# Low parts of two neighbouring ring slots in one VectorE operation, in the ten wide groups of a transformer layer pair

## What is computed

```python
h = sqrelu_mlp(rmsnorm(x, g), w1, w2)   # (256 x 8192) @ (8192 x 2048) is the second product
proj = h @ w_in                          # q, k, v: (256 x 2048) @ (2048 x 1024) each
```

## Time and profile before

| | |
|---|---|
| median of 3 runs | 1775.42 us |
| lowest, highest | 1775.01, 1775.8 us |
| span of the profiled execution | 1773.5 us |
| TensorE matmul busy | 1766.1 us |
| VectorE busy | 1277.0 us |
| ScalarE busy | 895.7 us |
| mean granted TensorE clock | 1.000 |

### The profile page before, as it was taken

One profiled execution on the slowest core, in us unless ns is written; L12 is line 12 of the kernel. 1 busy time (PEld: TensorE's weight loads), 2 busy tenths in 40 slices (PEclk: granted clock), 3 DMA queues, 4 the chain that ended last, 5 costly groups with the idle time before them and its releaser, 6 DMA issues.

```text
span 1773.5 us, 26289 instructions
## 1 busy us (share of the span) xinstructions
PE 1766.1 (100%) x8791; PEld 1497.5 (84%) x8791; DVE 1277.0 (72%) x1689; ACT 895.7 (51%) x1248; POOL 139.2 (8%) x190
## 2 busy tenths in 40 slices
PE   9999999999999999999999999999999999999999
PEld 7888888888888888888888887878888888888887
DVE  6567777556788788878887877898888655555654
ACT  7434444446556445545554455767644445553442
POOL 1012122000001000100000000020013011100000
PEclk9999999999999999999999999999999999999999
DMA  9564444555467656855775576565655554555554
GB/s 329 200 223 162 163 163 166 187 177 188 169 215 230 197 191 209 228 201 191 214 236 190 196 229 217 178 209 198 198 186 175 196 178 178 177 177 189 179 190 154
DMA packets 99116, 347.30 MB, mean 196 GB/s; under 512 B 11472, under 2 KB 11872, under 8 KB 98656
## 3 DMA queue, kind: packets, MB, share of 16 engines
q1 hardware_dynamic: 93392, 333.23, 54.8%
q0 software_dynamic: 4784, 12.60, 3.3%
q10 hardware_dynamic: 864, 0.44, 0.1%
HBM read 336.77 MB, written 2.11 MB: 191 GB/s over the span
## 4 chain that ended last, share of the span: by engine, by line
PE 95%; DVE 3%; ACT 1%; DMA 1%; issue 0%; POOL 0%; SPq 0%; ACTq 0%; DVEq 0%
PE bank L474 32%; PE bank L453 23%; PE bank L458 12%; PE bank L768 7%; PE bank L769 7%; PE bank L770 7%; PE bank L490 1%; DVE w_lo L1530 1%; PE bank L524 1%; DMA raw<-in_stream 1%; PE bank L646 1%; PE bank L661 1%; PE bank L603 0%; ACT w_hi L987 0%; PE bank L652 0%; PE bank L645 0%
## 5 line engine op out<-in xcount | busy, mean ns | idle before, releaser
L1530 DVE TENSOR_TENSOR w_lo<-raw,w_hi 128x1024 fp32r<-128x1024 f32 x620 | 753.5, 1224 | 372.9 <-ACT w_hi L987 368.9
L987 ACT ACTIVATE w_hi<-raw 128x1024 fp32r<-128x1024 f32 x620 | 648.2, 1055 | 580.2 <-PE bank L474 267.9
L453 PE MATMUL bank<-h_both,w_hi 128*128 128x512 f32 x1792 | 432.6, 393 | 0.0
L453 PEld LDWEIGHTS bank<-h_both,w_hi 128*128 128x128 f32 x1792 | 330.4, 188 | 65.4
L474 PE MATMUL bank<-w_hi,h_both 128*128 128x512 f32 x1160 | 361.6, 393 | 0.0
L474 PEld LDWEIGHTS bank<-w_hi,h_both 128*128 128x128 f32 x1160 | 215.7, 188 | 43.6
L458 PEld LDWEIGHTS bank<-h_both,w_lo 128*128 128x128 f32 x1792 | 229.7, 191 | 8.7
L458 PE MATMUL bank<-h_both,w_lo 128*128 128x256 f32 x1792 | 232.5, 283 | 0.0
L474 PE MATMUL bank<-w_lo,h_both 128*128 128x512 f32 x580 | 226.1, 390 | 0.0
L474 PE MATMUL bank<-w_hi,a_both 128*128 128x512 f32 x576 | 178.4, 391 | 0.0
L474 PEld LDWEIGHTS bank<-w_lo,h_both 128*128 128x128 f32 x580 | 108.9, 188 | 22.9
(11 more groups left out here) (278 smaller groups left out, 1784.0 us busy)
## 6 DMA issues: line engine op xcount, KB each, us to landing
raw<-in_stream SPq DMA_DIRECT2D x622, 512.0 KB, 3.3
wide<-scaled POOLq DMA_DIRECT2D x21, 256.0 KB, 4.8
res<-in_x SPq DMA_DIRECT2D x4, 512.0 KB, 7.4
rowg<-in_norm_rows POOLq DMA_DIRECT2D x2, 1024.0 KB, 9.0
gate<-cum_rows POOLq DMA_DIRECT2D x1, 2048.0 KB, 8.1
out<-wide SPq DMA_DIRECT2D x8, 256.0 KB, 4.3
wide<-gate POOLq DMA_DIRECT2D x7, 256.0 KB, 8.6
gate<-in_x_turned SPq DMA_DIRECT2D x5, 256.0 KB, 6.4
```

Source lines behind the costliest of these rows:

```text
L453: pe.matmul(tile_sum[b][:, :], w_hi[:, slot + half, k * P:(k + 1) * P], h_both[:, 8 * half + k, :], start=half == 0 and k == 0, stop=False)
L987: nc.scalar.activation(w_hi[:, slot, :], raw[:, slot, :], ACT.Copy).then_inc(hi_ready, 1)
L1530: nc.vector.tensor_tensor(w_lo[:, slot, :], raw[:, slot, :], w_hi[:, slot, :].bitcast(F32), ALU.subtract).then_inc(lo_ready, 1)
```

## The change

A function `rest_pair` makes the low parts of two neighbouring slots in one subtraction of 2048 columns. It waits until the high parts of both are made, and adds two to `lo_ready` at its end. In `wide_step` it replaces the two loops, and in `wide_join` the two `rests`. Nothing else is changed: the order of the operations on VectorE stays.

```diff
+            def rest_pair(c, slot):
+
+                dve.wait_ge(hi_ready, c + (RING + 2))
+                nc.vector.tensor_tensor(w_lo[:, slot:slot + 2, :], raw[:, slot:slot + 2, :],
+                                        w_hi[:, slot:slot + 2, :].bitcast(F32), ALU.subtract).then_inc(lo_ready, 2)
+
...
                 if drain:
                     drain(1, 0)
                     drain(1, 1)
-                for k in range(2):
-                    rest(c + at - RING + k, (at + k) % RING)
+                rest_pair(c + at - RING, at % RING)
                 form_rest(step, forms)
-                for k in range(2, 4):
-                    rest(c + at - RING + k, (at + k) % RING)
+                rest_pair(c + at - RING + 2, at % RING + 2)
 
             def wide_join(c, w, seven, part):
 
-                rests(c + 12, range(2))
+                rest_pair(c + 12, 0)
                 join_seven(w, seven, part)
-                rests(c + 12, range(2, RING))
+                rest_pair(c + 14, 2)
```

## The result

| | before | after |
|---|---|---|
| median of 4 runs each, on one chip | 1775.57 us | 1805.91 us |
| lowest, highest | 1775.01, 1775.8 | 1803.78, 1808.35 |
| span of the profiled execution | 1773.5 | 1802.9 |
| mean granted TensorE clock | 1.000 | 0.997 |

The change makes the kernel slower by 30.3 us: ratio 1.0172, 95% interval 1.016 to 1.0184. The direction and the mechanism were forecast. The median lies inside the range of 1781 to 1809, but 11 us above the 1794.5 that was predicted. The profiled execution took 1804.58 us, 1.7 more than its span.

A forecast was written before the change was run, and what follows sets the result against it. TensorE was taken to bound the kernel, with VectorE's saving hidden. Entries 3.4, plain links 8 and three links beside POOL's additions 8 sum to 19.4 us, giving 1794.5 us; range 1781 to 1809.

The forecast's parts named there:

- What bounds the kernel: Whole kernel: TensorE is busy 1766.1 of 1773.5 us, so VectorE's saving of 5 us is hidden and worth 0.
- The operation: Low-part subtraction on VectorE: one of 2048 columns takes 2.29 us, against 2.35 for two singles back to back.
- The second leg: VectorE's cycle, from the differences' start to the next pair's end: 5.74 us.
- The entries: Place 4 of group 0 and place 8 of group 7: TensorE waits 1.5 and 1.9 us, 3.4 in all.
- The 16 plain links: Links away from POOL's additions: cycle 10.74 us against TensorE's 10.2, so 0.5 us at each, 8 us in all.
- The load leg: From the pair's end until the second load has landed and differences start: 5.0 us, ends 4.58 and 5.71.
- the 0.37: In the time from pair's end to differences: the queue issues the second load 0.37 us after the first.
- the prediction's estimate from it: Loads after a pair: second lands 1.2 us after the first's 3.3, about 4.6 after the pair; sum +13.
- The three links beside POOL's additions: Places 8 and 9 of groups 1, 3 and 5: TensorE waits 1.8, 3.1 and 3.1 us, 8 in all.
- a rival of its own: TensorE's clock could fall to half behind 3 us waits, 10 us each; three give +49, 1825; chance 0.04.
- nothing of their own: Pairs of slots 2 and 3 and of the join have several microseconds to spare at TensorE: cost 0.
- TensorE's busy time: Sign in the changed profile: it stays near 1766 us while waits for the low part rise to some 19.

The follow-up runs named there:

- Experiment 1: Changed kernel with each low-part pair as two 1024-column operations, both still behind the second high part and released together at the end: 1805.55 us.
- Experiment 9: Kernel before, but SyncE's queue issues the load of slot 0 only when slot 1 is free, and slot 2 with slot 3: 1777.53 us.
- experiment 6: Changed kernel with POOL's four accumulating DMAs cut from 512 to 8 columns each: 1796.27 us.
- experiments 4 and 5: Kernel before with some pairs merged: the former only those of slots 2 and 3 in the steps, 1776.64 us; the latter only the join's two, 1777.35 us.
- (2): Changed kernel with single 1024-column operations that both wait for the second high part, but each releases its own slot: 1782.75 us.
- (8): Kernel before, but TensorE waits for both low parts of a pair of places before its first product: 1780.2 us.
- 3: Kernel before with only the pairs of slots 0 and 1 in the steps merged: 1796.68 us.

## Why the prediction came out as it did

**What bounds the kernel** was read rightly. VectorE gave 4.9 us back, at most 5 were forecast, and they were worth nothing. Experiment 1 shows it from the other side: with single operations the same +30.

**The operation**: 2.294 us, 2.29 taken. **The second leg** of the cycle: 5.73 us measured, 5.74 taken.

**The entries**: 3.2 us measured, 3.4 forecast.

**The 16 plain links**: 9.5 us, 8 forecast; 13 of them at 0.7 us each where 0.5 was taken, and three at nothing, behind the slow clock. The load leg is 5.20 us in the mean, from 4.75 to 6.09, where 5.0 was taken. The mis-sized term is the 0.37 that was added to today's 4.58 for the issue of the second load: the second issue starts 0.59 us after the first (the rows at 732.63 and 733.22), where the earlier trace rows had 0.37 at the opening. From its own issue the second load lands after 4.28 us in the mean before and 4.36 after, so its own time hardly changed. Of the 0.66 us by which the leg grew, from 4.54, 0.59 is thus the place behind the first issue. Experiment 9 measures the same leg without the rest of the change (5.18).

The Trainium skill (DMA: Bandwidth & Descriptors, the part on the two cost components) fits DMAs issued by GpSimd, not by SyncE as here; the prediction's estimate from it had the second load land 1.2 us behind the first and 4.6 us after the pair. In these 16 links the second lands 1.20 to 2.20 us behind the first, half of them within 1.34. So the trace comes near to that part. But the first lands 3.7 us after the pair in the mean, where 3.3 was taken, and the second 5.1; there the trace does not agree, and the measurement decides.

**The three links beside POOL's additions**: 13.7 us, 8 forecast. This is the main error. The load leg was sized well for groups 3 and 5 (7.09 and 7.97 against 7.6) and too short for group 1 (7.38 against 6.3), and experiment 6 gives 9.4 us for all the DMAs together. What was missing is the clock. The prediction had it as a rival of its own at a chance of 0.04, with 10 us for each fall, and left it out of the forecast. It came in each of the three links, and cost 1.5 to 1.6 us each, 4.7 in all, since the lower level held for eight matmuls and not for a cycle of 45. So both the chance and the price of that rival were wrong, in opposite directions. Without the 4.7 the three links are 9.0. At the rival's price three falls would have ended at 1825, outside the range. That they were cheap enough for the median to stay inside is luck.

**Elsewhere**: 2.6 us where nothing was forecast. 1.1 is at the start of group 9, where TensorE now waits for the additions of the join (the row with `gate` in the waits above), 0.7 is at place 4 of group 9, and the rest is in small amounts at the first steps of the other groups. The prediction said that the pairs of slots 2 and 3 and those of the join cost nothing of their own; experiments 4 and 5 give +1.45, which does not exclude nothing, and +2.0, which just does. "Nothing of their own" was too strong for the join.

**TensorE's busy time** was forecast to stay near 1766 and is 1777.1. The slow matmuls are 4.7 us of it. A matmul's record is 0.39 us where the next begins 0.23 later, so the last one before each of 17 waits shows up to 0.16 more, 2.7 us. The other 3.6 are not accounted for. Busy time of this engine is thus not a measure to 1% of work done; the spacing of its matmuls is.

**Why the parts don't add up.** The late second high part costs 7.6 us alone (2), the late loads 2.1 (9), TensorE's late start 4.9 (8), and all together 30. The cycle explains it. TensorE needs 10.2 us. Before the cycle is 9.56 (4.54 + 5.02). With late loads alone it is 10.20, and just hides. With the wait alone it is about 10.4 (4.65 + 5.73), 0.2 over. With both it is 10.9, 0.7 over, at nearly every link. TensorE also enters the links without room: at place 4 of the groups behind group 0, other than 7, it starts 0.15 to 0.25 us after the pair's end, where it started 2.0 to 2.4 us after the first low part's end before, and 1.2 to 1.4 with the wait alone. Each part first uses up the same 0.6 us of room in the cycle and the same room at place 4, and what is beyond them is paid at 16 of the 19 links.

**What stays open** is what makes the clock fall. In the changed kernel the wait of 2.34 us at 732.60 is followed by a fall (above). This one, at place 8 of group 7, is longer and is not; its next matmuls are 0.23 us apart:

```profile
1182.70 0.47 PE L768 MATMUL bank<-w_hi,h_both 128*128 128x512 f32 x1 [2.53 <-DVE w_lo L1540]
```

In group 5, behind 3.23 us, TensorE is slow from its first matmul on, in groups 1 and 3 only some 1.2 to 1.5 us later. All runs of the changed kernel and of experiment 1 have the lower mean clock (0.996 to 0.997). In the profiled executions of 3 and 6 it is 1.000, with waits of up to 2.5 us; it is 0.997 to 0.999 in the other runs of 3, and 0.999 in one other of 6. So the length of one wait does not settle it, and no run here separates it from what surrounds the wait.

## What to carry to other kernels

In a ring of buffers, an operation's end is a release, and joining two operations joins two releases. Before merging, follow the cycle once round (release, issue, landing, each step, release) and compare it with the time that the bounding engine needs for the same work: here 0.6 us of room in the cycle hid most of each part of the change alone (+2 to +8 us), and their sum crossed it at 16 of 19 links (+30). What the merge saves on an engine that is not the bound, 5 us here, is worth nothing against that.

## What the runs showed of the hardware

- Two loads of 512 KB released together are issued 0.59 us apart (0.92 us for both issues) and let the differences start 5.2 us after the release. With releases 1.13 us apart, they start 4.54 after the second. So the delay is 0.66 us, and the second issue's place behind the first is 0.59 of it; from its own issue the second load lands after 4.28 us before and 4.36 after. Issue times of both loads were not varied by themselves.
- Two subtractions of 1024 columns back to back take 2.35 us, one of 2048 takes 2.29. The Trainium skill (VectorE: DVE Perf Modes, the DRAIN section) says that the next operation does not start until the pipe is empty, but also that "a next op that is not held starts earlier". The rows agree with the latter: two of 1.224 us would be 2.45 one behind the other, so about 0.1 is hidden, and a merge saves 0.06 us.
- TensorE's clock fell to its lower level for only some 3.4 us at a time (granted clock 0.75 and 0.83 in the two stretches of 4 us above), once even after 1.5 us of matmuls at the full level behind the wait. A fall cost 1.5 to 1.6 us of matmul time, and by the estimate above about 1 us of the kernel's.
